# Hybrid encoder step with a mixture of 32 experts: the two units of four experts run right behind the fixed pairs

## The reference, cut to what matters

```python
g_val, g_idx = lax.top_k(p_group, 1)            # one of 4 groups
e_val, e_idx = lax.top_k(p_exp, TOP_K)          # 2 of the 8 experts in it
for gi in range(N_GROUPS):
    h = jax.nn.silu(jnp.einsum('md,edf->mef', xt, w_e1[gi])) * jnp.einsum('md,edf->mef', xt, w_e3[gi])
    out = out + jnp.einsum('mef,efd->md', h * combine[:, gi, :, None], w_e2[gi])
```

## Time and profile before

| | us |
|---|---|
| median of 3 runs | 903.25 |
| lowest, highest | 899.1, 903.4 |
| the profiled execution | 896.7 |
| its span in the trace | 894.9 |
| first hidden step of the experts (start) | 617.83 |
| last result step ends | 847.6 |

### The profile page before, as it was taken

How to read it: one execution, slowest core, us unless ns; L and a number is a source line. 1 busy time by engine, 2 the same in 40 slices (tenths; PEclk the granted TensorE clock), 3 DMA queues, 4 the chain that set the end, 5 groups by cost and what they waited for, 6 DMA issues and landing times.

```text
span 894.9 us, 11842 instructions
## 1 busy us (share of the span) xinstructions
PE 764.7 (85%) x4700; PEld 555.0 (62%) x4700; DVE 364.2 (41%) x632; ACT 232.7 (26%) x449; POOL 157.7 (18%) x157
## 2 busy tenths in 40 slices
PE   6999999999799999999999999945999978295700
PEld 6999984774466999999999945432333333031200
DVE  4899927997676401110111023374111101010168
ACT  5214231736576522221222200030111101010100
POOL 4000001000313353334333300012011110000100
PEclk9999999999899999999999999965999999696955
DMA  8423225031100722222222087481999999999762
GB/s 327 138 78 94 77 71 190 12 68 38 45 1 14 305 86 81 83 94 84 83 83 84 1 346 313 174 328 51 376 419 424 425 420 426 425 424 424 306 249 82
DMA packets 33202, 173.36 MB, mean 194 GB/s; under 512 B 6472, under 2 KB 7032, under 8 KB 24824
## 3 DMA queue, kind: packets, MB, share of 16 engines
q1 hardware_dynamic: 28232, 161.30, 46.8%
q0 software_dynamic: 4912, 11.28, 3.4%
HBM read 162.07 MB, written 16.78 MB: 200 GB/s over the span
## 4 chain that ended last, share of the span: by engine, by line
PE 74%; DMA 14%; DVE 8%; issue 2%; ACT 1%; SPq 0%; POOLq 0%; ACTq 0%; DVEq 0%
PE PS L658 38%; DMA expert<-in_w_e 12%; PE PS L959 9%; PE PS L850 7%; PE PS L641 5%; PE PS L979 3%; PE PS L768 2%; PE PS L734 2%; PE PS L748 2%; PE PS L716 2%; DVE x_tiles L1688 1%; PE PS L811 1%; PE PS L914 1%; DVE x_tiles L1700 1%; PE PS L868 1%
## 5 line engine op out<-in xcount | busy, mean ns | idle before, releaser
L658 PE MATMUL PS<-x_hi,w_hi 128*128 128x288 f32 (+2 forms) x656 | 141.3, 297 | 9.4 <-DVE x_lo L1297 8.6
L959 PE MATMUL PS<-expert,moe_tmp 128*64 128x512 f32 (+2 forms) x576 | 116.3, 650 | 38.4 <-DMA expert<-in_w_e 37.1
L658 PE MATMUL PS<-x_lo,w_hi 128*128 128x288 f32 (+2 forms) x656 | 141.0, 297 | 0.0
L658 PE MATMUL PS<-x_hi,w_lo 128*128 128x288 f32 (+2 forms) x656 | 141.0, 297 | 0.0
L1042 ACT ACTIVATE w_hi<-raw_ring 128x1024 fp32r<-128x1024 f32 (+1 forms) x57 | 57.0, 1001 | 212.6 <-PE PS L658 207.2
L658 PEld LDWEIGHTS PS<-x_hi,w_hi 128*128 128x128 f32 x656 | 105.7, 190 | 9.7 <-POOL w_lo L461 8.6
L658 PEld LDWEIGHTS PS<-x_lo,w_hi 128*128 128x128 f32 x656 | 105.8, 190 | 0.0
L658 PEld LDWEIGHTS PS<-x_hi,w_lo 128*128 128x128 f32 x656 | 105.8, 190 | 0.0
L959 PEld LDWEIGHTS PS<-expert,moe_tmp 128*64 128x64 f32 (+2 forms) x576 | 38.9, 137 | 105.7 <-issue 103.8
L461 POOL TENSOR_TENSOR w_lo<-raw_ring,w_hi 128x1024 fp32r<-128x1024 f32 (+1 forms) x33 | 70.7, 2144 | 133.8 <-ACT w_hi L1042 133.8
L1314 DVE SCALAR_TENSOR_TENSOR conv_z<-attn_tmp,wdw,conv_z 128x576 f32<-128x576 f32 x120 | 90.6, 811 | 0.3
(11 more groups left out here) (286 smaller groups left out, 1027.0 us busy)
## 6 DMA issues: line engine op xcount, KB each, us to landing
expert<-in_w_e SPq DMA_DIRECT2D x32, 2048.0 KB, 24.7
expert<-in_w_e SPq DMA_DIRECT2D x32, 1024.0 KB, 30.8
raw_ring<-in_w_gate_t SPq DMA_DIRECT2D x24, 512.0 KB, 3.4
raw_ring<-in_w_glu_t SPq DMA_DIRECT2D x8, 512.0 KB, 4.7
raw_ring<-in_w_como_t SPq DMA_DIRECT2D x8, 512.0 KB, 3.5
heads<-in_w_out SPq DMA_DIRECT2D x1, 4096.0 KB, 14.0
x_rows<-x_tiles SPq DMA_DIRECT2D x8, 512.0 KB, 5.1
expert_out<-expert_rows SPq DMA_DIRECT2D x8, 512.0 KB, 7.2
```

What stands on the lines that cost most here:

```text
L658: mm = pe.matmul(half(name, s, 128, cols[s]), w[:, n % 2, at + 128 * k:at + 128 * k + 128], x[:, k, t0[s]:t0[s] + cols[s]], start=(k == 0 ...
L959: mm = pe.matmul(PS[r0:r0 + nr, 2, :].rearrange("p (s f) -> p s f", s=2), xgT[:, k, r0:r0 + nr], w13[s % NB][:, :, k, :], start=(k == 0), ...
```

## The change

One line: the order in which the units run.

```diff
-UNIT_ORDER = (2, 3, 4, 5, 0, 6, 7, 8, 10, 1, 11, 9)
+UNIT_ORDER = (10, 11, 2, 3, 4, 5, 0, 6, 7, 8, 1, 9)
```

## The result

The changed kernel takes **904.98 us** in the median of 10 runs (902.12 to 907.93), the kernel before, run beside it, 899.89 us (896.39 to 903.4). The ratio is 1.006, with a 95% interval of 1.0042 to 1.0077: slower by 0.6%, 5.1 us. The forecast was +5.3 us. The absolute forecast of 908.5 stood on a median of three runs, 903.25, which turned out 3.4 us above the median of ten.

The account below looks back on a forecast made before the run. The expert part was taken as bound by one full DMA stream of weights. TensorE's later end, +5.4 us (replacing +3.6, not added), on the 903.25 median gave 908.6, stated as 908.5; range 903.0 to 912.0.

Parts of the forecast that it names:

- Part 1: Stage 3, now a unit of four: its last up load lands 2.6 us before the stage starts; price 0.
- Part 2: Stage 4, now a unit of four: hidden step waits 19.7 us, result step another 20, both off the path.
- Part 3: Load queue near 700 us: stays busy although a load waits for hidden 4; 2.9 us margin, price 0.
- Part 4: End of the stream: three down loads instead of five behind the last up load, so TensorE ends 3.6 us later.
- Part 5: Stages 12 to 14: hidden 12 waits some 4.2 us, then takes 8.8; +5.4 us in all, replacing the +3.6.
- No clock loss: Rival at hidden 12: it runs at full speed after its wait; +3.7 us, 907.0; chance 0.26.
- Late downs: Rival at the stream's end: downs come later behind the last up load, which lands earlier; +1 to +2, 904.7; chance 0.12.
- A gap: Rival near 700 us: a load issued too late leaves the stream idle; 911.5, up to 914 with a second; chance 0.15.
- Faster: Rival over the whole weight stream: it drains at a rate 5% above 424 GB/s; 897; chance 0.07.

Follow-up runs that it names:

- the run with 14 fillers: Changed kernel with 14 matmuls of constants ahead of hidden step 11 and 14 ahead of hidden step 12; ratio 1.0037 against the kernel before.

## Why the prediction was right, point by point

The working is that of the prediction; each measure is from the first load at 627.39 there and at 629.82 in the changed kernel.

- **Part 1** (stage 3 with four experts costs nothing): right, hidden 3 at 655.48 without a wait.
- **Part 2** (hidden 4 waits for U13, result 4 for D13): right, 20.0 us for 19.7, hidden 4 took 9.37 for 9.1 to 9.5. Result 4 starts at 99.0 from the first load; the prediction had 98.6.
- **Part 3** (the queue doesn't run dry): right in the outcome, the engines stay full at 415 and 434 GB/s on both sides of 700. The margin was mis-sized: 2.9 us in the prediction, 1.7 to 1.8 in the two runs that pushed hidden 4 back. The end of the queued work was right, D11 at 72.0 for 72.1 from the first load in both of these runs. The missing 1.1 us are three terms: hidden 4 ended at 67.1 and not at 66.7 in the changed kernel (0.4), U16 was issued 0.2 behind it, and a restart of the empty queue cost 3.0 and not 2.5. For that last term: U28 lands 115.6 and 115.4 us behind U16's issue in the two runs, and without a gap at 184.5, 112.5 behind D11's 72.0.
- **Part 4** (three downs behind U31): right. U31 lands at 838.07, 208.3 from the first load, predicted 208.2, before 202.8. D31's landing isn't in this trace; the changed kernel once more has it at 215.7, the run with 14 fillers at 216.3, for 216.4 forecast, so U31 lands 7.6 and 8.1 ahead of it for 8.2. That 3.8 us behind the last byte is the least, as the prediction had it, the last load in two halves shows to be a little too much: 3.4 there. The run with two downs moved ahead shows the mechanism by itself, and the run with 14 fillers shows the size that the order has alone: 3.4 us for 3.6.
- **Part 5** (U28, hidden 12, half clock): right. Hidden 12 starts at 184.7 for 184.4, takes 8.78 for 8.8, but waits 3.22 for 4.2; hidden 14 starts at 210.1 for 210.2; the end is at 225.4 for 225.6. Switched off by fillers, the clock is worth 1.8 us for 1.7. One thing was wrong without a cost: hidden 11 lost to the clock too, behind a wait of 3.24, where the prediction had it at full. Hidden 12 waited for U28 anyway. The argument for the clock loss was weaker than it was put: 4.2 us was to lie above the row of 3.31, and the wait was below it. In the runs waits of 1.90 to 2.54 went both ways, and all from 2.92 on paid, so the term came true with less to spare than the prediction says.
- **The rivals.** *No clock loss* has the right size (223.6 measured with the fillers) and the wrong case. *Late downs* needed a smaller distance between U31 and the end. *A gap* didn't come, and the two runs that forced it cost what it was said to cost, us for us: hidden 4 ends 9.0 apart in them, and the lengths are 8.9 apart. *Faster*: the rate stayed at 421 to 424 GB/s in long stretches.
- **The absolute time** was 3.5 us too high, 3.4 of it from the three runs of before. From the same runs comes the line of 907.8, above which the prediction would call the kernel slower: the measured 904.98 lies below it, and beside ten runs of before it is slower all the same, by 0.6%.

What stays open: how much of the 3.4 us either of the two loads, U28 and U31, would cost without the other in the changed order. Their paths meet within 0.2 us, and only U31's was measured by itself, in the old order.

## What to carry to other kernels

Where loads run in one queue that is always full, the last byte is fixed (D31 landed at 215.7 to 216.5 in the five traces without a gap that have it) and the order decides only what stands behind it: for each of the last loads, add the work that follows it on the engine to the time that it lands, and take the latest. Put the large piece with the long work behind it early in the queue, and leave many small loads with little work behind them for the end. That advice is drawn from the four other orders of units, all slower than the one of before; a better order was not found here. An engine that waits 20 us ahead of a step and 19 us behind it may still have under 2 us of slack in that step, if the step frees the buffers for the next loads.

## What the runs showed of the hardware

TensorE's half clock didn't go by the length of the wait alone. A hidden step of a pair took 8.79 us behind a wait of 1.90 in the run with units 1 and 8 exchanged, and 7.09 behind 2.15 in the run with one unit of four early; in the changed kernel once more it took 7.09 behind 2.54:

```profile
783.33 7.09 PE L959 MATMUL PS<-expert,moe_tmp 128*64 128x512 f32 x32 [2.15 <-DMA expert<-in_w_e]
...
795.77 7.09 PE L959 MATMUL PS<-expert,moe_tmp 128*64 128x512 f32 x32 [2.54 <-DMA expert<-in_w_e]
```

Behind waits of 2.92 to 6.27 it took 8.42 to 9.97, in every case seen; behind waits of 1.69 and less it took 7.09. In the long waits of the changed kernel the granted clock fell to 0.50, the lower of its two levels; the 0.57 of the stretch from 710 to 728 is a mean that has a piece at the upper one:

```profile
715.00:728.00 13.00, 0.00 (x0) 0.00 (x0) 0.00 (x0) 0.00 (x0) 0.00 (x0) 0.50 1.02 426
```

And matmuls of constants in the wait, up to 0.3 us before the weights came, kept the step behind them at 7.09; with 1.34 us between them and the weights, ahead of hidden 11 in the run with 14 fillers, they did too.
